# Reordering the opening of a two-layer decoder trunk on one core: row-wise squares, eight chunk places, late branch parameters

## What is computed

```
cond = jax.nn.silu(c)
for l in range(DEPTH):                                     # DEPTH = 2
    ada = (cond @ w_ada[l] + b_ada[l]).reshape(bsz, 9, D_MODEL)
    u = modulate(h, norm_pre[l, 0], ada[:, 0], ada[:, 1])  # rmsnorm(h) * g * (1 + scale) + shift
    y = swiglu(u, ffn1_w_up[l], ffn1_w_down[l])            # 1024 -> 2 x 2816 -> 1024
    h = h + 0.5 * ada[:, 2][:, None, :] * rmsnorm(y, norm_post[l, 0])
    ...                                                    # mixer, then the second feed-forward
```

## Time and profile before

| | |
|---|---|
| device time, median of 3 runs | 2857.78 us (2849.29 to 2859.83) |
| the profiled execution, its own time | 2865.7 us |
| its span in the profile | 2863.7 us |
| TensorE busy | 2724.2 us, 95% of the span |
| VectorE, ScalarE, GpSimd busy | 1356.8, 1040.4, 366.6 us |
| granted TensorE clock, mean | 0.948 of full speed |
| HBM read | 303.44 MB, 107 GB/s over the span |

### The profile page before, as it was taken

How to read it: one execution, slowest core, us unless ns; L and a number is a source line. 1 busy time by engine, 2 the same in 40 slices (tenths; PEclk the granted TensorE clock), 3 DMA queues, 4 the chain that set the end, 5 groups by cost and what they waited for, 6 DMA issues and landing times.

```text
span 2863.7 us, 34634 instructions
## 1 busy us (share of the span) xinstructions
PE 2724.2 (95%) x12963; PEld 2265.9 (79%) x12963; DVE 1356.8 (47%) x2051; ACT 1040.4 (36%) x1232; POOL 366.6 (13%) x148
## 2 busy tenths in 40 slices
PE   8899998999988989999999999999998889899998
PEld 8788887987866777888878888798777667788886
DVE  4777326753244348633268752377142443643322
ACT  1433313644244334333243332345332543343312
POOL 0100002213311330000010000221331123100000
PEclk6899999999988999999999999999997899899998
DMA  5675332222141225433237632322223112243221
GB/s 189 195 231 191 103 98 75 68 73 89 59 89 45 74 74 184 156 101 100 91 116 234 225 118 101 90 69 67 89 89 59 59 59 74 85 136 103 88 103 44
DMA packets 268422, 306.94 MB, mean 107 GB/s; under 512 B 17783, under 2 KB 245499, under 8 KB 268324
## 3 DMA queue, kind: packets, MB, share of 16 engines
q1 hardware_dynamic: 268172, 305.23, 33.7%
q10 hardware_dynamic: 152, 0.35, 0.0%
HBM read 303.44 MB, written 2.45 MB: 107 GB/s over the span
## 4 chain that ended last, share of the span: by engine, by line
PE 88%; DVE 5%; ACT 2%; issue 2%; POOL 1%; DMA 1%; SPq 1%; POOLq 0%; ACTq 0%; DVEq 0%
PE bank L610 25%; PE bank L612 24%; PE bank L611 24%; PE bank L837 1%; PE bank L1144 1%; PE bank L838 1%; PE bank L839 1%; PE bank L624 1%; PE bank L720 1%; PE bank L1035 1%; ACT w_both_hi L1194 1%; PE bank L1000 1%; POOL w_both_lo L2380 1%; DVE smax L2129 1%; POOL cross L2353 1%
## 5 line engine op out<-in xcount | busy, mean ns | idle before, releaser
L610 PE MATMUL bank<-u_hi,w_both_hi 128*128 128x512 f32 x2032 | 813.1, 400 | 24.5 <-issue 10.3
L611 PE MATMUL bank<-u_lo,w_both_hi 128*128 128x512 f32 x2032 | 801.6, 395 | 0.0
L612 PE MATMUL bank<-u_hi,w_both_lo 128*128 128x512 f32 x2032 | 801.1, 394 | 0.0
L1622 DVE TENSOR_TENSOR w_both_lo<-raw,w_both_hi 128x2048 fp32r<-128x2048 f32 x149 | 342.9, 2301 | 622.6 <-ACT w_both_hi L1194 622.0
L1194 ACT ACTIVATE w_both_hi<-raw 128x2048 fp32r<-128x2048 f32 (+1 forms) x203 | 386.0, 1902 | 665.5 <-PE bank L612 665.4
L610 PEld LDWEIGHTS bank<-u_hi,w_both_hi 128*128 128x128 f32 x2032 | 388.7, 191 | 119.8 <-issue 19.6
L612 PEld LDWEIGHTS bank<-u_hi,w_both_lo 128*128 128x128 f32 x2032 | 387.8, 191 | 83.8
L611 PEld LDWEIGHTS bank<-u_lo,w_both_hi 128*128 128x128 f32 x2032 | 388.8, 191 | 78.5
L2380 POOL TENSOR_TENSOR w_both_lo<-raw,w_both_hi 128x2048 fp32r<-128x2048 f32 x54 | 249.9, 4628 | 757.0 <-ACT w_both_hi L1194 757.0
L610 PE MATMUL bank<-g_hi,w_both_hi 128*128 (+1 forms) x704 | 276.2, 392 | 0.0
L612 PE MATMUL bank<-g_hi,w_both_lo 128*128 (+1 forms) x704 | 274.0, 389 | 0.0
(11 more groups left out here) (359 smaller groups left out, 3313.4 us busy)
## 6 DMA issues: line engine op xcount, KB each, us to landing
raw<-in_ffn_w_up SPq DMA_DIRECT2D x88, 1024.0 KB, 5.1
ada_w<-in_w_ada SPq DMA_DIRECT2D x64, 1024.0 KB, 5.1
raw<-in_w_in SPq DMA_DIRECT2D x52, 1024.0 KB, 5.2
raw<-in_ffn_w_down SPq DMA_DIRECT2D x44, 1024.0 KB, 4.9
raw<-in_w_branch SPq DMA_DIRECT2D x12, 1024.0 KB, 5.1
first_ada_w<-in_w_ada SPq DMA_DIRECT2D x8, 1024.0 KB, 11.5
raw<-in_w_out SPq DMA_DIRECT2D x8, 1024.0 KB, 5.0
raw<-in_s_w_glu SPq DMA_DIRECT2D x4, 1024.0 KB, 5.0
```

The source lines that it names most:

```text
L610: pe.matmul(dst, hi, rhi, start=first, stop=False)
L611: pe.matmul(dst, hi, rlo, start=False, stop=False)
L612: return pe.matmul(dst, lo, rhi, start=False, stop=last)
L1622: v.tensor_tensor(w_lo[s][:, :], raw[s][:, :], w_hi[s][:, :].bitcast(F32), SUB).then_inc(lo_split[s].sem, 1)
```

## The change

The opening is reordered on four engines. The sums of squares are taken token by token from `x_tok` on ScalarE (a square with an accumulated sum, four instructions of 1024 elements), so the squares of `h`, the sums of TensorE and their slots go. ScalarE also copies tiles 4 to 7 of `h`. All eight chunks of `w_ada` have places of their own; the first four are queued right behind `x_tok`, ahead of the row loads. TensorE multiplies chunks 1, 4 and 6 directly, VectorE prepares chunks 0, 2, 3 and 5, and chunk 7 is divided, a half each. The first two weight chunks are queued between chunks 5, 6 and 7, and their remainders are written by VectorE in place of GpSimd. The derivation of the branch parameters (now `step_sizes`, `magnitudes`, `factors`, `lambda_sums`, `lambdas`) moves into the down stage of the first feed-forward, between the splits, and with it ScalarE's two sines and one exponential. The arithmetic of the parameters is the same.

```diff
+FIRST_BY_PE, FIRST_BY_VEC = (1, 4, 6), (0, 2, 3, 5)
-        first_ada_w = [shared(f"first_ada_w{s}", k, [P, KT, ADA_WIDTH]) for s, k in enumerate((32, 50, 58, 66, 74, 82))]
+        first_ada_w = [at(f"first_ada_w{n}", 16 + 8 * n, [P, KT, ADA_WIDTH]) for n in range(4)] + \
+            [shared(f"first_ada_w{n}", 18 + 8 * n, [P, KT, ADA_WIDTH]) for n in range(4, ADA_AHEAD)]
+        x_sq = shared("x_sq", 90, [P, 2, D_MODEL])
...
 # SyncE
-            sp.dma_start(onehot[:, :], bucket_onehot).then_inc(line_loaded, 16)
-            sp.dma_start(rel33[0:NUM_BUCKETS, :], rel_bias).then_inc(line_loaded, 16)
+            for n in range(4):
+                load_first_ada(n)
             for l in range(DEPTH):
...
-            for n in range(ADA_AHEAD):
-                if n >= 6:
-                    sp.wait_ge(first_column, n - 5)
-                load_ada(first_ada_w[n % 6], first_ada_loaded[n % 6], 0, n * ADA_WIDTH)
+            for n in range(4, 6):
+                load_first_ada(n)
+            sp.dma_start(onehot[:, :], bucket_onehot).then_inc(line_loaded, 16)
+            sp.dma_start(rel33[0:NUM_BUCKETS, :], rel_bias).then_inc(line_loaded, 16)
+            load_first_weights(0)
+            load_first_ada(6)
+            load_first_weights(1)
+            load_first_ada(7)
...
 # TensorE
-            for m in range(KT):
-                pe.wait_ge(h_squared, m + 1)
-                if m == 0:
-                    begin_sums(TB)
-                for b in range(TB):
-                    i = pe.matmul(sums[:, b:b + 1], sq_buf[:, m % SQ_SLOTS, b * P:(b + 1) * P], sum_w[:, 0, 0, 0:1],
-                                  start=False, stop=m == KT - 1 and b == TB - 1)
-                i.then_inc(h_sq_summed, 1)
-            pe.wait_ge(inverses_ready, 1)
-            rstd_rows(TB)
+            first_columns(FIRST_BY_PE[1])
+            pe.wait_ge(line_loaded, 32)
+            pe.wait_ge(h_loaded, 4)
+            pe.matmul(bank[2][0:N_MAPS, :], rel33[:, :], onehot[:, 0:SEQ], start=True, stop=True).then_inc(line_made, 1)
+            pe.matmul(bank[3][0:N_MAPS, 0:P], rel33[:, :], onehot[:, SEQ:LINE], start=True, stop=True).then_inc(line_made, 1)
+            for i in range(3):
+                summed_columns(i)
+            first_columns(FIRST_BY_PE[2])
+            summed_columns(3)
+            n = ADA_AHEAD - 1
+            first_columns(n, (1,))
+            pe.wait_ge(first_ada_step, (len(FIRST_BY_VEC) + 1) * KT)
+            pe.matmul(bank[7][:, 2 * n:2 * n + 1], first_ada_acc[4][:, 0:P], ones[:, 0:1], start=True, stop=True).then_inc(first_column, 1)
...
 # ScalarE
+            act.wait_ge(x_loaded, 16)
+            for b in range(TB):
+                if b >= 2:
+                    st.wait(back=1)
+                st.did(act.activation(x_sq[:, b % 2, :], x_tok[:, b, :], ACT.Square, scale=D_MODEL ** -0.5, accum_out=h_ms[:, b:b + 1]))
+            st.wait()
+            act.activation(roots[:, TB:], h_ms[:, :], ACT.Sqrt, bias=EPS_COL).then_inc(roots_ready, 1)
+            for m in range(4, KT):
+                act.wait_ge(x_turned, m + 1)
+                act.activation(h[:, m, :], bank[m if m < 6 else m - 6][:, :], ACT.Copy).then_inc(h_by_act, 1)
...
 # VectorE, the down stage of the first feed-forward
+                if L == 0 and f == 0:
+                    step_sizes()
+                    split(L, (c1 + 3) % 2, (c1 + 3) // 2 + 1)
+                    magnitudes()
+                    split(L, (c1 + 4) % 2, (c1 + 4) // 2 + 1)
+                    factors()
+                    lambda_sums()
+                    split(L, (c1 + 3) % 2, (c1 + 3) // 2 + 2)
+                    lambdas()
+                    split(L, (c1 + 4) % 2, (c1 + 4) // 2 + 2)
+                with v.Fori(0 if L or f else 2, (FT // 2 - 3) // 2) as j:
...
 # VectorE, the opening
+            for i, n in enumerate(FIRST_BY_VEC):
+                v.wait_ge(first_ada_loaded[n], 16)
+                weighted_sum(first_ada_w[n], first_ada_acc[i][:, :], lambda k: v.wait_ge(first_ada_step, i * KT + k), first_ada_step)
+                if i == 2:
+                    place_vectors()
...
+            split(0, 0, 1)
+            split(0, 1, 1)
+            v.wait_ge(first_ada_loaded[ADA_AHEAD - 1], 16)
...
 # GpSimd
-            split_low(0, 0)
-            split_low(0, 1)
```

More of the change, by code:

```diff
@@ L347, in build @@
         ada_loaded = [signal(f"ada_loaded{s}", 16 * sum(ADA_ROUNDS)) for s in range(3)]
[L348 removed]
+        first_ada_loaded = [sem(f"first_ada_loaded{n}") for n in range(ADA_AHEAD)]
         first_ada_step, first_column = sem("first_ada_step"), sem("first_column")
@@ L1465, in _ @@
-            act.wait_ge(h_sq_summed, KT)
-            act.activation(roots[:, TB:], sums[:, 0:TB], ACT.Sqrt, bias=EPS_COL).then_inc(roots_ready, 1)
-            split(0, 0, 1)
-            split(0, 1, 1)
             modulate(0)
@@ L1781, in all_vectors @@
-                phase, mag, f_re, f_im = part(V_PHASE), part(V_MAG), part(V_FRE), part(V_FIM)
-                lre, lim, lst = part(V_LRE), part(V_LIM), part(V_LSTEP)
-                R = [pscr[:, i] for i in range(12)]
-                def do(ins):
-                    ins.then_inc(vec_steps, 1)
-                    steps[0] += 1
-                    v.wait_ge(vec_steps, steps[0])
-                def ts(o, a, s1, s2, op0, op1):
-                    do(v.tensor_scalar(o, a, s1, s2, op0, op1))
@@ L2145, in _ @@
             v.memset(rel33[NUM_BUCKETS:NUM_BUCKETS + 1, :], MASKED).then_inc(const_ready, 1)
-            for m in range(KT):
+            for m in range(4):
                 v.wait_ge(x_turned, m + 1)
-                v.tensor_copy(h[:, m, :], bank[m if m < 6 else m - 6][:, :]).then_inc(h_loaded, 1)
-            steps = all_vectors()
-            v.wait_ge(const_ready, 4)
-            for i in range(4):
-                rows = slice(32 * i, 32 * i + 32)
-                v.tensor_copy(same_ch[rows, :], ident[rows, rows]).then_inc(vec_steps, 1)
@@ L2155, in _ @@
-            steps += 4
-            v.wait_ge(cond_ready, 1)
-            for n in range(3):
-                v.wait_ge(first_ada_loaded[3 + n], 16)
-                weighted_sum(first_ada_w[3 + n], first_ada_acc[n][:, :], lambda k: v.wait_ge(first_ada_step, n * KT + k), first_ada_step)
-            v.wait_ge(first_column, ADA_AHEAD)
+                v.tensor_copy(h[:, m, :], bank[m][:, :]).then_inc(h_loaded, 1)
+            v.wait_ge(roots_ready, 1)
+            v.reciprocal(rstd_pair[:, TB:], roots[:, TB:]).then_inc(inverses_ready, 1)
@@ new lines, in _ @@
+            v.wait_ge(cond_ready, 1)
+            for i, n in enumerate(FIRST_BY_VEC):
[3 more added lines that the diff above has]
+                    place_vectors()
+                    v.wait_ge(const_ready, 4)
+                    for a in range(4):
+                        rows = slice(32 * a, 32 * a + 32)
+                        counted(v.tensor_copy(same_ch[rows, :], ident[rows, rows]))
@@ L2163, in _ @@
             st.wait()
-            v.wait_ge(vec_steps, steps)
             pre(0, 0)
             st.wait()
-            v.wait_ge(line_copied, 2)
-            v.wait_ge(const_ready, 4)
-            v.wait_ge(roots_ready, 1)
-            st.did(v.tensor_copy(h_ms[:, :], sums[:, 0:TB]))
-            v.reciprocal(rstd_pair[:, TB:], roots[:, TB:]).then_inc(inverses_ready, 1)
+            v.wait_ge(h_by_act, 4)
             v.wait_ge(h_rstd_ready, 1)
```

143 lines of the change are left out of this document (85 added, 58 removed).

## The result

| | before | changed |
|---|---|---|
| device time, median | 2857.78 us (2849.29 to 2860.89, 5 runs) | 2834.59 us (2826.38 to 2844.26, 5 runs) |
| the profiled execution: its time, its span | 2865.7, 2863.7 us | 2833.33, 2831.3 us |
| its mean granted clock | 0.948 | 0.956 |

The ratio of the times is 0.9925, with a 95% interval of 0.9896 to 0.9955. The change makes the kernel 23.2 us faster by the medians; the prediction said 25.2 and 2832.6 us. It is a gain of 0.75%, and the interval leaves it between 0.45% and 1.04%.

What follows compares the result with a forecast made beforehand. TensorE, busy 2724.2 of 2863.7 us, was taken as the bound, with recoverable time in the opening's waits. Gains 2.85 + 15.46 + 6.85 = 25.2 took 2865.7 to 2840.5, less 7.9 for the median: 2832.6 us; range 2820 to 2846.

Steps and rivals of the forecast that it cites:

- The mark: Start of the feed-forward's sixteenth product, at 86.56 us before; whatever moves it was to move the kernel's end.
- columns, end from 56.25: Opening: TensorE's column products were to end at 53.4 in place of 56.25 us, 2.85 us gained.
- squares, 15.96 us to 0.5: Opening, from the columns' end to the first modulated tile: sums, root and spreading go, 15.46 us gained.
- first tiles, 14.35 us to 7.5: First modulated tile to sixteenth product: remainders already written by VectorE, so TensorE waits less, 6.85 us gained.
- branch parameters in the down stage: First feed-forward's down stage: 15.6 us of VectorE work was to cost nothing, covered by TensorE's multiplying.
- The queue of loads: SyncE's queue in the opening: chunk 4 was to be issued at 22.0 and land at 30.4 us.
- the two bounds: Opening, chunk 4's time to land: 5.1 us gives 27.1, 8.35 us gives 30.4; the latter was taken.
- the first rival: Opening's queue: small loads wait for the chunks, chunk 4 lands at 39.4, columns shift 9.0 us; 2841.6 us, 17%.
- The clock rival: Opening: TensorE's clock rises during the columns, passes cost 6.4 us less; 2826.2 us, 8%.
- the third term: First modulated tile to sixteenth product: VectorE's remainders, written under the columns, cut the interval to 7.5, gaining 6.85 us.
- The fourth rival: First rounds of the feed-forward: the dense run stays at 1.2 GHz, costing 60 us; 2892.4 us, 3%.
- the slow case: First rounds of the feed-forward at 1.2 GHz: 279 dearer products cost 60 us; 2892.4 us, 3%.

Runs made afterwards that it cites:

- e3: Changed kernel with the branch parameters, ScalarE's sines and exponential included, back in the opening behind VectorE's third weighted sum; 2842.84 us.
- e4: Changed kernel with the first two remainders given back from VectorE to GpSimd; 2839.08 us.
- e1: Kernel before with only the squares taken token by token on ScalarE and TensorE's 33 matmuls of squares removed; 2836.88 us.
- e5: Changed kernel with the 20 row loads and two broadcasts issued by ScalarE at its start in place of SyncE; 2827.95 us.
- e9: Changed kernel with row loads and broadcasts issued by ScalarE, plus six unused wide products in TensorE's idle time before the first product; median 2830.41 us, ratio 0.9901.
- e6: Changed kernel with unused wide matmuls before every second column matmul of chunks 4, 6, 7, behind each sum, and 49 ahead of chunk 4; 2839.46 us.
- e7: Changed kernel with unused wide matmuls before every fourth column matmul of chunks 4, 6, 7, behind each sum, and 49 ahead of chunk 4; 2836.27 us.

## Why the prediction was right

The mark moved by 24.03 us against a sum of 25.2. The prediction's terms, against the same intervals of the two traces:

| term | predicted | measured |
|---|---|---|
| columns, end from 56.25 | 2.85 | 1.67 (end at 54.58) |
| squares, 15.96 us to 0.5 | 15.46 | 15.51 (55.03 - 54.58 = 0.45 left) |
| first tiles, 14.35 us to 7.5 | 6.85 | 6.85 (62.53 - 55.03 = 7.50 left) |
| branch parameters in the down stage | 0 | 0 (root 24.08, mark 24.03) |

*The queue of loads.* Chunk 4 was to be issued at 22.0 and to land at 30.4, and did so at 22.79 and 31.20. Between the two bounds, 5.1 and 8.35 us, the upper was right: 8.36. The four chunks were issued by 11.95, sooner than the 13.6 of the prediction; the 22 small loads then took 10.76 us in place of 8.4. The difference between these two, 2.4 us, is the first row load, which took 2.83 us to issue where its fellows took 0.25 to 0.42: it stood behind four chunks, and the queue held it. That is the mechanism of the first rival. It held one small load and not all 22, for 2.4 us where the rival had 9.0, and as the chunks themselves had been issued 1.65 us sooner, only 0.8 us of it reached chunk 4. TensorE waited for the rows' data until 24.36, which cost nothing, as chunk 4 came later still.

*The columns.* 98 passes were put at 21.0 us and took 21.16, 0.216 each; the bias line at 2.0 and took 2.23. The clock rival is refuted for this kernel: the granted clock stayed at 0.50. The claim that TensorE and not VectorE is last held, VectorE's half sum ending at 51.25. That this is its bound of 51.2 is luck: the remainders ended 1.3 us later than reckoned (48.33 against 47.0), and the half sum took 1.3 us less than its upper value (2.9 against 4.2). e3 and e4 show how thin that margin is: 2.9 us, and either of two edits of the change, undone, uses it up.

*The clock after the columns.* It rose early in the dense run, between 60.5 and 61, near where the earlier trace rows had led the prediction to put it. That the third term came out at 6.85 to the hundredth is luck all the same, since the fifteen products it contains vary by 1.3 us with the moment of the rise. The fourth rival had nothing for it in any execution.

*The attribution* of the third term needs a correction that the total hides. The prediction gave the 6.85 us to VectorE's taking over the remainders. In e1, where GpSimd keeps them, the first tile comes at 57.42 and the mark at 65.61, so the interval is 8.19 us and 6.16 of the 6.85 us are there already. From the tile to the first product it takes 2.39 us, exactly as in the changed kernel; the remaining 0.69 lie in the fifteen products (5.80 us against 5.11), where the clock rose later, so the whole term is there. It belongs to the root's earlier place, which lets ScalarE's split go ahead. What the move to VectorE saves is the 1.5 us at the first product that e4 shows. The prediction had the mechanism right, a VectorE held up by GpSimd, and credited its end to the wrong clause of the change; the forecast didn't depend on which, since both were in it.

*The median.* The prediction took the profiled execution's distance from its median, 7.9 us, off again. Without this step it would have said 2840.5. The profiled execution of the kernel before lay above all five of its timed ones (2849.29 to 2860.89), the changed kernel's 1.3 us below its own median; so the two profiles differ by 32.4 us where the medians differ by 23.2, and the step was needed. What makes one execution 7 us longer than another behind the first root can be read in the traces. Between the first and the last of these roots every one of the eleven has the same 10900 matmuls. They keep TensorE busy for 2272.04 us before, 2261.63 in the changed kernel, 2270.77 in e3, which is the longest of the others, and 2259.29 in e5. The stretches at the 1.2 GHz level in there add up to some 212, 188, 208 and 184 us. The same work takes longer where the clock is low for longer; why it is low for longer in one execution stays open.

*Small slips*, none of which moves the forecast: the first rival has the chunks land near 22.7, where the text ahead of it has 21.3; the slow case's 60 us on top of 2832.6 are 2892.6 and not 2892.4; ScalarE's sines and exponential with their table took about 1.8 us in the kernel before, not 1.7.

## What to carry to other kernels

Before crediting a stall to the engine that is slow in it, ask why its work starts so late: here a split stood behind a root in one engine's program, and moving the root cured a collision between two other engines. A queue that issues many small loads is itself a resource; when the DMA engines go idle behind it, another engine should issue the small ones, and the order within the one queue matters little (0.3 us here, against 5.4). A mean over a row of instructions can hide one that was held: seven of 0.98 us each were one of 4.5 and six of 0.36. And when a step must hide behind another, write down the margin: 2.9 us here, of which two harmless-looking edits each took all.

## What the runs showed of the hardware that was not expected

- One-column passes alone can run at the full clock for a while. Chunk 1's 32 passes, right behind the transposes, took 3.63 us, 0.113 each, at a granted clock of 1.00; the clock was 0.50 from 20 us on, after TensorE had begun to wait. The prediction had 0.149 as the nearest estimate for such a pass.

```profile
15.51 3.63 PE L1148 MATMUL bank<-cond,first_ada_w 128*128 128x1 f32 x32
```

- In the changed kernel TensorE was busy without a gap from 31.20 to 54.58 at a granted clock of 0.50. In e9 the low level ended with the first real product: six wide bf16 products began at 49.17, and from 52.59 a product took 0.23 us. The Trainium skill, "TensorE: Matmul & The Clock Gate", section "What's actually happening", says that the engine's activity releases the throttle. If busy time is taken for activity, the first of these rows does not agree with it, as the prediction held; the second, with its wide products, does. In e6 and e7 the clock fell from 1.00 to 0.50 (at about 39.8 and 36.5) with TensorE busy up to the fall and no idle time of it since before 34 us.
- A VectorE instruction with two large inputs in SBUF that meets a 128x2048 GpSimd instruction ends 0.2 to 0.6 us behind the end of the latter, however short it is by itself: 4.52 us in place of 0.36 (e4), 2.71 and 4.25 in place of 0.75 (kernel before). `mod_buf`, with one such input and a bank, kept its 0.75 us beside GpSimd.
- The issue of a small load behind four 1 MB chunks took 2.83 us (changed kernel), and that of `onehot` behind two more chunks 3.62 us, at 23.90. On ScalarE's queue, with the same chunks in flight from SyncE, the 22 small loads took 0.27 to 0.64 us each.
